# Eighteen gated output tiles transposed by DMA in 16-bit halves instead of on TensorE, and two pieces of the plan moved one block sooner

## The reference

```python
    h = ((h - mu) * lax.rsqrt(var + EPS)).reshape(b_, s_, MIX_A) * head_norm_g.astype(f32)
    y_a = h.astype(x.dtype) * jax.nn.silu(z_a)
...
    return x + jnp.concatenate([y_a, y_b], axis=-1) @ w_out
...
        branch = jnp.concatenate([mix_out, mem_out], axis=-1) * jax.nn.silu(gate)
        x = x + branch @ w_out[i]
```

## Time and profile before

| | |
|---|---|
| median of three runs | 3303.74 us (3303.61 to 3304.02) |
| the profiled execution: time | 3303.69 us |
| its span in the trace | 3301.9 us |
| PE busy | 3290.7 us |
| DVE busy | 2086.1 us |
| ACT busy | 1674.3 us |
| DMA | 617 MB, mean 187 GB/s |

### The profile page before, as it was taken

The page is one execution under the profiler, slowest core; times in us unless marked ns, Lnnn a source line. Parts: engine busy times, 40 slices in busy tenths (PEclk is TensorE's granted clock), DMA queues, the critical chain, the costliest instruction groups (busy, mean ns, idle before and its releaser), DMA issues.

```text
span 3301.9 us, 39899 instructions
## 1 busy us (share of the span) xinstructions
PE 3290.7 (100%) x15454; PEld 2742.7 (83%) x15454; DVE 2086.1 (63%) x2843; ACT 1674.3 (51%) x2274; POOL 172.7 (5%) x241
## 2 busy tenths in 40 slices
PE   9999999999999999999999999999999999999999
PEld 7888888888888888888888888888888888888887
DVE  6557655756757755657667665665555667757664
ACT  5544444546654444546655454454444545555443
POOL 2000000000000000000000000000000321200000
PEclk9999999999999999999999999999999999999999
DMA  8665655565555665565556555555556555565554
GB/s 271 211 200 174 196 182 182 191 191 179 177 182 179 191 184 180 185 200 171 190 192 224 175 191 182 171 168 182 185 179 191 167 174 178 186 212 184 168 183 172
DMA packets 314621, 617.35 MB, mean 187 GB/s; under 512 B 20988, under 2 KB 23364, under 8 KB 314048
## 3 DMA queue, kind: packets, MB, share of 16 engines
q1 hardware_dynamic: 301808, 581.05, 55.2%
q0 software_dynamic: 10336, 27.45, 2.7%
q10 hardware_dynamic: 2288, 6.30, 0.5%
HBM read 608.10 MB, written 6.62 MB: 186 GB/s over the span
## 4 chain that ended last, share of the span: by engine, by line
PE 95%; DVE 2%; ACT 2%; issue 1%; DMA 0%; SPq 0%; DVEq 0%; ACTq 0%
PE acc L1602 29%; PE acc L1604 29%; PE acc L1603 29%; PE tr L1689 2%; ACT weights_hi L890 1%; DVE work L1174 1%; PE nm L1792 1%; DVE weights_lo L1170 1%; ACT work L901 1%; PE tr L1671 0%; PE tr L1604 0%; PE tr L1603 0%; PE tr L1602 0%; PE tr L1780 0%; DVE work L1438 0%
## 5 line engine op out<-in xcount | busy, mean ns | idle before, releaser
L1170 DVE TENSOR_TENSOR weights_lo<-weights_raw,weights_hi 128x1024 fp32r<-128x1024 f32 x1103 | 1344.4, 1229 | 957.9 <-ACT weights_hi L890 953.3
L890 ACT ACTIVATE weights_hi<-weights_raw 128x1024 fp32r<-128x1024 f32 x1103 | 1165.0, 1059 | 1148.8 <-PE acc L1604 1113.8
L1602 PE MATMUL acc<-weights_hi,u_hi 128*128 128x512 f32 x3136 | 1239.8, 395 | 1.5 <-DVE weights_lo L1170 1.5
L1604 PE MATMUL acc<-weights_hi,u_lo 128*128 128x512 f32 x3136 | 1223.0, 390 | 0.0
L1603 PE MATMUL acc<-weights_lo,u_hi 128*128 128x512 f32 x3136 | 1221.4, 389 | 0.0
L1602 PEld LDWEIGHTS acc<-weights_hi,u_hi 128*128 128x128 f32 x3136 | 588.9, 188 | 125.4 <-issue 4.0
L1604 PEld LDWEIGHTS acc<-weights_hi,u_lo 128*128 128x128 f32 x3136 | 588.6, 188 | 123.9
L1603 PEld LDWEIGHTS acc<-weights_lo,u_hi 128*128 128x128 f32 x3136 | 589.1, 188 | 118.9
L1602 PE MATMUL acc<-weights_hi,y_hi 128*128 128x512 f32 x1280 | 502.7, 393 | 2.5 <-DVE y_lo L1174 1.5
L1604 PE MATMUL acc<-weights_hi,y_lo 128*128 128x512 f32 x1280 | 498.7, 390 | 0.0
L1603 PE MATMUL acc<-weights_lo,y_hi 128*128 128x512 f32 x1280 | 498.2, 389 | 0.0
(11 more groups left out here) (267 smaller groups left out, 1882.6 us busy)
## 6 DMA issues: line engine op xcount, KB each, us to landing
weights_raw<-in_w_in_dram SPq DMA_DIRECT2D x384, 512.0 KB, 3.6
weights_raw<-in_w_out_dram SPq DMA_DIRECT2D x256, 512.0 KB, 4.3
weights_raw<-in_a_w_in_dram SPq DMA_DIRECT2D x176, 512.0 KB, 4.3
weights_raw<-in_b_w_in_dram SPq DMA_DIRECT2D x112, 512.0 KB, 3.6
weights_raw<-in_c_w_in_dram SPq DMA_DIRECT2D x112, 512.0 KB, 4.3
weights_raw<-in_w_mem_kv_dram SPq DMA_DIRECT2D x63, 512.0 KB, 4.8
kv_scratch<-work ACTq DMA_DIRECT2D x8, 512.0 KB, 4.8
qk_tiles<-in_w_a_dram POOLq DMA_DIRECT2D x8, 512.0 KB, 4.4
```

The costliest lines, as they stand in the source:

```text
L890: SC_E.activation(WH[:, b % RING], RAW[:, b % RING], ACT.Copy).then_inc(sem("hi_done"), 1)
L1170: V.tensor_tensor(WL[:, b % RING], RAW[:, b % RING], WH[:, b % RING].bitcast(F32), ALU.subtract).then_inc(sem("lo_done"), 1)
L1602: T.matmul(dst, hi_l, hi_r, start=start, stop=False, **kw)
L1604: return T.matmul(dst, lo_l, hi_r, start=False, stop=stop, **kw)
```

## The change

For eighteen of the 24 gated output tiles (p = 0 to 2 of the mLSTM in both layers, the memory attention of all four layers, groups 0 and 1 of the mixer in all four layers), the piece `tp` is replaced by three pieces:

- `apart`, in the slot where `tp` stood: ACT copies the 256 x 512 tile as 16-bit words, the even words (one half of each f32) to one side and the odd words to the other.
- `turn`, eight slots on in SP's list: SP waits for `half_in` and issues one transposing DMA of 128 x 2048 words, 512 KB, SBUF to SBUF.
- `join`, five slots after `apart`: ACT waits for the DMA, puts the two halves of each element together again (two copies of 1,024 words per partition), and then makes the high part from SBUF; DVE makes the low part from SBUF.

The six other tiles of that kind keep `tp`. DVE's pieces that overwrite `O` wait for `half_in` also. Buffers are free places of `work` and `qk_tiles`. Besides, the last of the four memory-row tiles at the start goes one slot sooner (slot 11 instead of 12), and so do, for p = 1 to 3, the linear recurrence's pieces from `cvs` to `lrs`.

```diff
+ISSUE, JOIN = 8, 5
...
+    def apart(slot, src, ready, buf):
+
+        q = pl.piece(slot, "apart", src=src, ready=ready, buf=buf)
+        pl.piece(slot + ISSUE, "turn", at=q, buf=buf)
+        return q
+
+    def xbar(slot, src, ready, dst, kt0, gain, buf):
+
+        q = apart(slot, src, ready, buf)
+        return pl.piece(slot + JOIN, "join", dst=dst, kt0=kt0, gain=gain, at=q, buf=buf)
...
-        mem_tp.append(tp(FIRST - 1 if j == 0 else FIRST + 4 * j - 2, "x%d" % j, ("x_in%d" % j, 16), "y", 4 * j,
+        mem_tp.append(tp(FIRST + (-1, 2, 6, 9)[j], "x%d" % j, ("x_in%d" % j, 16), "y", 4 * j,
...
-            ya.append(tp(s + 8, "o", ("mf_out", mf), "y", 4 * p, ("par", l * NPAR + HG + 4 * p, 1)))
+            gain = ("par", l * NPAR + HG + 4 * p, 1)
+            ya.append(tp(s + 8, "o", ("mf_out", mf), "y", 12, gain) if p == 3 else
+                      xbar(s + 8, "o", ("mf_out", mf), "y", 4 * p, gain, "m"))
...
-            c += 4 if p == 0 else 3
+            c += 4 if p == 0 else 2
...
-            return tp(s + 4, "o", ("fi_out", fi), "y", 4 * grp, ("par2", CS, 0) if late else None)
+            gain = ("par2", CS, 0) if late else None
+            return (tp(s + 4, "o", ("fi_out", fi), "y", 8, gain) if grp == 2 else
+                    xbar(s + 4, "o", ("fi_out", fi), "y", 4 * grp, gain, "a" if kind == "A" else "b"))
...
-                ts.append(tp(pl.here() + 4, "o", ("sv_out", sv), "y", 4 * grp, None))
+                ts.append(tp(pl.here() + 4, "o", ("sv_out", sv), "y", 8, None) if grp == 2 else
+                          xbar(pl.here() + 4, "o", ("sv_out", sv), "y", 4 * grp, None, "a"))
...
+                for p in pl.at[n]:
+                    if p.kind == "turn":
+                        wait(sp, "half_in", p.at)
+                        sp.dma_start_transpose(turned(p.buf), halves(p.buf)).then_inc(sem("half_t_" + p.buf), 16)
...
+                    elif k == "apart":
+                        ref(act, p.ready)
+                        if p.same:
+                            act.wait_ge(sem("half_t_" + p.buf), 16 * p.nth)
...
+                            wait(act, "jn_lo", last.get(("join", p.buf)))
+                        for t in range(2):
...
+                            i = SC_E.activation(halves(p.buf)[:, 2 * CH * t:2 * CH * t + 2 * CH].rearrange(
+                                "p (s f) -> p s f", s=2), src.bitcast(U16).rearrange("p (f s) -> p s f", s=2), ACT.Copy)
+                        i.then_inc(sem("half_in"), 1)
+                    elif k == "join":
+                        act.wait_ge(sem("half_t_" + p.buf), 16 * (p.at.nth + 1))
+                        for t in range(2):
+                            to = joined(p.buf)[:, :, P * t:P * t + P].bitcast(U16).rearrange("p f (k s) -> p s f k", s=2)
+                            i = SC_E.activation(to, turned(p.buf)[:, 8 * t:8 * t + 8].rearrange("p (s f) k -> p s f k", s=2),
+                                                ACT.Copy)
+                        i.then_inc(sem("half_out"), 1)
...
```

More of the change, by code:

```diff
@@ L20 @@
 F32R = mybir.dt.float32r
+U16 = mybir.dt.uint16
 ALU = mybir.AluOpType
@@ L100, in __init__ @@
                  bank=None, gives=None, at=None, pt=None, ms=None, to=None, form=None, par=0, emptied=None,
-                 order=None, times=None, twin=None):
+                 order=None, times=None, twin=None, buf=None):
         self.kind = kind
@@ L114, in __init__ @@
         self.mode, self.bank, self.gives = mode, bank, gives
-        self.times, self.twin = times, twin
+        self.times, self.twin, self.buf = times, twin, buf
         self.form, self.par, self.emptied, self.order = form, par, emptied, order
@@ L132 @@
            "gt": "gt_out", "zb": "zb_out", "ge": "ge_x", "ox": "ox_out"}
-TIMES = {"tp_pe": 2, "tp_hi": 2, "tp_lo": 2, "ge_o": 2, "ge_x": 2, "ge_y": 2, "ge_t": 2}
+ISSUE, JOIN = 8, 5
+TIMES = {"jn_hi": 2, "jn_lo": 2, "tp_pe": 2, "tp_hi": 2, "tp_lo": 2, "ge_o": 2, "ge_x": 2, "ge_y": 2, "ge_t": 2}
 class Plan:
@@ L224, in close @@
                 last[p.kind] = p
+                p.nth = count.get((p.kind, p.buf), 0)
+                count[p.kind, p.buf] = p.nth + 1
+                p.same = last.get((p.kind, p.buf))
+                last[p.kind, p.buf] = p
         return self
@@ L233, in tp @@
         return pl.piece(slot, "tp", src=src, ready=ready, dst=dst, kt0=kt0, gain=gain)
+    def apart(slot, src, ready, buf):
[5 more added lines that the diff above has]
+        return pl.piece(slot + JOIN, "join", dst=dst, kt0=kt0, gain=gain, at=q, buf=buf)
     def tiles(pieces, signal="tp_lo", where=(0, 2, 4, 6)):
         if signal == "tp_lo":
-            return {i + h: (signal, p, h) for i, p in zip(where, pieces) for h in range(2)}
+            return {i + h: ("jn_lo" if p.kind == "join" else signal, p, h) for i, p in zip(where, pieces)
+                    for h in range(2)}
         return {i: (signal, p) for i, p in zip(where, pieces)}
@@ L610, in program, with halves, turned, joined @@
         DECAY = sb("lru_decay", [P, 2, 16])
+        APART = {"u0": (W, 8464, 9488), "u1": (W, 10512, 11536), "q": (W, 4612, 12560), "m": (W, 10512, 11536),
+                 "a": (W, 6656, 7680), "b": (QKB, 0, 1024)}
+        def halves(buf):
+            t, a, _ = APART[buf]
+            return t[:, a:a + 1024].bitcast(U16)
+        def turned(buf):
+            t, _, b = APART[buf]
+            return t[:, b:b + 1024].bitcast(U16).rearrange("p (b k) -> p b k", k=P)
+        def joined(buf):
+            t, a, _ = APART[buf]
+            return view(t, a, 4, S)
         at = [0]
@@ L935, in _ @@
                         i.then_inc(sem("sq_out"), 1)
+                    elif k == "apart":
+                        ref(act, p.ready)
+                        if p.same:
+                            act.wait_ge(sem("half_t_" + p.buf), 16 * p.nth)
+                        if p.buf == "q":
+                            wait(act, "mo_out", last.get("mo"))
+                            act.wait_ge(sem("kv_st"), 16 * 8)
+                            act.wait_ge(sem("tb_st"), 16)
+                        else:
+                            wait(act, "jn_lo", last.get(("join", p.buf)))
+                        for t in range(2):
+                            src = (XT[:, t] if p.src == "xt" else O[:, t] if p.src == "o" else
+                                   X[:, t, CH * int(p.src[1]):CH * int(p.src[1]) + CH])
+                            i = SC_E.activation(halves(p.buf)[:, 2 * CH * t:2 * CH * t + 2 * CH].rearrange(
[8 more added lines that the diff above has]
+                        i.then_inc(sem("half_out"), 1)
+                        wait(act, "half_out", p)
+                        wait(act, "mm_done", p.used.get(p.dst))
+                        hi, x = ACTS[p.dst][0], joined(p.buf)
+                        for h in range(2):
+                            j, k_ = 2 * h, p.kt0 + 2 * h
+                            if p.gain is None:
+                                i = SC_E.activation(hi[:, k_:k_ + 2], x[:, j:j + 2], ACT.Copy)
+                            elif p.gain[2] == 0:
+                                i = SC_E.activation(hi[:, k_:k_ + 2], x[:, j:j + 2], ACT.Copy, scale=param(p.gain, 0))
+                            else:
+                                for e in range(2):
+                                    i = SC_E.activation(hi[:, k_ + e], x[:, j + e], ACT.Copy, scale=param(p.gain, j + e))
+                            i.then_inc(sem("jn_hi"), 1)
@@ L1236, in _ @@
                                 i.then_inc(sem("tp_lo"), 1)
+                    elif k == "join":
+                        hi, lo = ACTS[p.dst]
+                        x = joined(p.buf)
+                        for h in range(2):
+                            half(dve, "jn_hi", p, h)
+                            for e in range(2):
+                                j = 2 * h + e
+                                hf = hi[:, p.kt0 + j].bitcast(F32)
+                                if p.gain is None:
+                                    i = V.tensor_tensor(lo[:, p.kt0 + j], x[:, j], hf, ALU.subtract)
+                                else:
+                                    i = stt(lo[:, p.kt0 + j], x[:, j], param(p.gain, j), hf, ALU.mult, ALU.subtract)
+                            i.then_inc(sem("jn_lo"), 1)
                     elif k == "rs":
@@ L1385, in _ @@
                             wait(dve, "tp_pe", last.get("tp"))
+                            wait(dve, "half_in", last.get("apart"))
                         for t, ps in enumerate((NMB, SCB)):
```

## The result

The changed kernel takes 3287.05 us in the median of six runs (3285.36 to 3287.45), the kernel before 3303.58 (3303.50 to 3304.02). The ratio is 0.9948, with a 95% interval of 0.9938 to 0.9958. That is 16.5 us less, where 17.7 had been forecast. The six runs lie at two levels, four at 3287.0 to 3287.5 with a mean clock of 0.999 and two at 3285.4 and 3285.6 with a clock of 1.0.

What follows compares the result with a forecast made beforehand. PE was taken as the bound, busy 3290.7 of 3301.9 us. 3303.7 - 15.7 (tiles) - 1.2 (start tile) - 1.0 (recurrence) = 3285.8, taken as 3286; own range 3282 to 3290, full range 3281 to 3303.

Steps and rivals of the forecast that it cites:

- What leaves PE: Eighteen output tiles lose their transposes on PE, 0.87 us each: 15.7 us gained, all on the path.
- What ACT gets costs nothing: ACT's added copies, 1.06 us each, leave it 2.4 us behind after a join, under 5.9: no PE wait, cost 0.
- The transfer: Transposing DMA on SP's queue: 6 us taken, hidden up to some 13 us at most joins, cost 0.
- The 9.6 us: Time a transfer has from its issue on SP before ACT, reaching the join, must wait for it.
- The tight place in A: A layers, memory join and group 0's apart share a slot: 7.5 us on ACT, 1.2 us left, cost 0.
- The moved pieces: Start's fourth memory tile one slot sooner, -1.2 us; recurrence pieces of p = 1 to 3 sooner, -1.0 us.
- the convolution's low half would be done just when PE comes to the gate product: Moved recurrence: low half done at 753.8, PE there at 753.9; set against 0.26 us gained, net -0.2 each.
- one of the signs of being wrong on record: Waits of PE at the gate product, listed among what would show the forecast wrong.
- B or C together: Rivals: 16-bit ACT copies of 2.1 us (3295), recurrence moves causing PE waits (3293); either 0.12; both within no-change rival, 0.09.
- the cost of 0 in part 2: ACT's extra copies at apart and join: 2.4 us behind is under 5.9, so PE does not wait.
- the 5.9 us that the weights allow: How late ACT and DVE together may be with a block's weight split before PE waits.

Runs made afterwards that it cites:

- the moves alone: Kernel before with only the memory tile in slot 11 and recurrence pieces one slot sooner, all tiles on PE: 3301.01 us, ratio 0.9991.
- the late join: Changed kernel with the join of layer C's memory tile 21 slots after its apart instead of 5: 3284.31 us, ratio 0.9941; timed again 3284.26 us.
- the sooner convolution: Kernel with C's memory join 21 slots after its apart, plus the convolution's second half in the first's slot for p = 1 to 3: 3286.67 us.
- the tile on PE: Changed kernel with layer C's memory tile back on TensorE, seventeen tiles by DMA: 3284.74 us.

## Why the prediction was right, and where it was off

- **What leaves PE** was right: 15.7 us forecast at 0.87 a tile. The starts of the blocks give 16.3 (0.90 to 0.91 each); the runs' 16.7 hold the end of the last store too.
- **What ACT gets costs nothing**: right at seventeen of the eighteen joins, wrong in C (below). The size was right (76 us forecast, 74 measured). The copies of `apart` take 1.05 us as the f32 copies of the same count, those of `join` 1.35 in the mean, with four strides on the writing side. ACT is 2.5 us behind after a join and is idle again two slots later.
- **The transfer**: 6 us taken, 6.7 measured. Its cost of 0 was right, but with less room than I gave it. I let SP reach the turn 2.3 us into slot s+1 and forgot that `apart` delays the split of that slot. The 9.6 us are 7.8, and what is left to spare at the first join is about 1.3 us. The run with the joins at three slots falls off that edge. Also missing was that SP itself is held 4.5 us by a transposing transfer. ACT's waits for weights from DMA rise from 26.1 us in 20 waits to 35.6 in 31, but PE's weight loads wait for `weights_lo` only once, 0.6 us at the start. So the hold did no harm that the trace shows.
- **The Trainium skill**, Advanced Engine Details and Errata, has both sentences, in X-Bar Transpose (TRN2) and in DGE: Hardware vs Software. Here 512 KB in 6.7 us are 78 GB/s, issue and latency included, where the plain loads of 512 KB from DRAM land in 3.7 to 4.8 us. This speaks against the equal speed that X-Bar Transpose (TRN2) states, at this size and beside this traffic. The sentence in DGE: Hardware vs Software ranks the hardware path below the software one, and no run here used the software path. Neither decides the kernel's time.
- **The tight place in A** was right: ACT begins the crowded slot at 1888.59 and ends the apart at 1896.37, 7.8 us against 7.5 counted, and PE does not wait. (By the terms on record the next low half is done at 9.8, not 9.7.)
- **The moved pieces**: the tile of the start 1.2 forecast, 1.4 measured; the recurrence 1.0 forecast, 1.5 measured. The step "the convolution's low half would be done just when PE comes to the gate product" named the right place, but it was priced at next to nothing: four waits of 0.8 us are there, one of the signs of being wrong on record. All six waits for the weights went, where I had a quarter us off each. Two terms too small by some 3 us each, one of gain (4.7 measured where 1.6 was counted) and one of loss (3.1 where nothing was), cancel, so it is luck that the sum came near. (Six times the 0.2 on record is also 1.2, not 1.0.)
- **What I missed** is in the rival section only as "B or C together". I looked for crowded slots in A and not in C, where the attention of group 0 begins in slot h-4, which is the slot of the memory join (in B it begins one slot later, and no wait of PE came of it). A late attention step, not the weight split, is what PE waited for. It costs 1.8 us, and 3.4 where the clock falls behind it; moving the join wins back 1.1 and 3.2. The step that had it wrong is the cost of 0 in part 2, which compares the delay of ACT only with the 5.9 us that the weights allow.
- **The total** came within 1.2 us of the forecast partly by luck. Measured, the terms are 16.3 for the tiles, 1.4 for the start, 1.5 for the recurrence, 1.0 behind the last store, and 1.8 lost in C: 18.4 us, as the runs at clock 1.0 show (3303.9 to 3285.4). The fall of the clock takes some 1.7 of it back in the others. 17.9 had been added up, with nothing for C, the clock and the store.

That PE's stand is what lets the clock fall is the pattern of all runs here: no run of a kernel without a long stand (the kernel before, the moves alone, the late join with and without the sooner convolution, the tile on PE) fell below 1.0. It is not shown further than that. Of the 18 runs whose only such stand is the one in C, 8 fell and 10 did not, and nothing on record tells them apart.

## What to carry to other kernels

When one engine sets the time and is never idle, work that leaves it is worth its full length here, and all the care belongs to the places where the work lands. List, for every slot that gets something new, what else stands in it on each engine: the small steps of a dependent chain (a head's softmax) have far less room than the prefetched weights. And count the way of the request too. A transfer's time runs from its issue, and the issue waits for whatever the new work itself delays.

## What the runs showed of the hardware that was not expected

- A transposing DMA of 128 x 2048 16-bit elements holds SP's queue for 3.3 to 4.9 us (an ordinary 512 KB load: 0.37) and lands after 5.4 to 8.3 us, 6.7 in the median. It is made of about 2,080 packets.
- ACT copies 1,024 16-bit elements per partition in 1.05 us with strided reading and 1.35 with the four-level strided writing of the join; the f32 copy takes 1.06.
- A single stand of PE of about 2 us, with matmuls back to back before it, was followed by some three us at the lower clock in 8 of 18 runs (1.7 to 2 us lost). With the joins at two slots, where twenty waits add up to 56 us, the mean clock fell to 0.993.
